# Picking the 256 best scores of a row: counting passes over the bits of the 256th score instead of rounds of eight maxima

## The chip, the cores and the metric

The kernel runs on one core of one Trainium2 chip. The metric is the device time of one execution in microseconds (us), the median of several. A core has a matrix engine (PE; its weight loads are listed as PEld), a vector engine (DVE), a scalar engine (ACT), a third elementwise engine (POOL) and a queue engine for transfers (SP). Each runs its own list of instructions in order; they meet at semaphores.

## The reference

One inference step of a two-layer encoder on 1024 new frames of one stream (the prompt) and 16 frames for each of 8 running streams (the sample; 2048 cached frames each). Layer 0 is a gated recurrence, layer 1 a sparse attention; both are followed by a feed-forward block. The change lies in the sparse attention. An indexer scores every key for every query, the best 256 keys of each query are kept, and ordinary attention runs over those:

```python
dots = jnp.einsum('bthd,bsd->bths', qib, ki_all, preferred_element_type=F32)
score = jnp.einsum('bth,bths->bts', wb.astype(F32), jax.nn.relu(dots))
score = jnp.where(admissible[None], score, -jnp.inf)
sel_val, sel_idx = lax.top_k(score, n_sel)          # n_sel = 256
valid = sel_val > -jnp.inf
...
logits = jnp.where(valid[:, :, None, None, :], logits, -jnp.inf)
p = jax.nn.softmax(logits, axis=-1).astype(vg.dtype)
```

A query of the prompt sees the keys of its own chunk of 64 frames and of the chunks before. `top_k` takes the lower index where scores tie.

## The kernel before, in words

The program is a chain of phases with a barrier between them: recurrence, feed-forward 0, projections, `select_phase`, `attend_prompt_phase`, `attend_sample_phase`, output projection, feed-forward 1, final norm. Queries lie on the 128 partitions. The prompt has 8 tiles of 128 queries, t = 0 to 7; tile t has (t+1)*128 keys. Tiles 0 and 1 have at most 256 keys and need no choice; tiles 2 to 7 do, and so does the sample, whose 128 queries have 2064 keys each (`score_s`). No key is gathered: the choice becomes an additive mask (`mask_p`, `mask_s`, 0 or a large negative number `NEG`), and attention runs over all keys.

**Choosing.** `top_step` is one step of the choice. A MAX8 finds the eight largest scores of each row, the next step replaces them by `TAKEN` (MATCH_REPLACE8), and so on; 64 steps (`STEPS`), 32 of each kind, mark 256 scores. `mask_from` turns the marks into the mask in one pass. Tiles go in pairs: (2,3) are `EARLY_TOP`, (4,5) and (6,7) are `LATE_TOP`, and the sample is alone. All of it runs on DVE.

**Where the steps stand in DVE's list.** In `select_phase` a loop over tiles 2 to 7 and 8 heads forms the prompt's scores: PE makes the dots (L1431 to L1433), ACT takes the relu into two buffers `se_relu_p` (L1476), DVE adds them up (L1533). In the 32 rounds of tiles 4 to 7 each round is followed by one step for the pair (2,3). After the loop DVE takes the remaining 32 steps of (2,3), their masks, and the first 8 steps of (4,5) (`LATE_STEPS_EARLY`), while PE and ACT score the sample (L1456, L1444, L1484, L1487), which needs nothing of DVE. The barrier follows. `attend_prompt_phase` starts with 6 more steps (`first_steps`) and then runs 64 blocks (tile t, pair of heads j), each of two halves: PE makes the logits (L1620 to L1622), DVE adds the mask and takes the row maximum (L1747, L1752, L1754), ACT takes the exponential (L1695), PE transposes (L1631), ACT copies (L1688), PE multiplies with the values (L1643), ACT scales (L1702, needs the reciprocal of DVE, L1737). PE keeps one half in hand: the logits of half u may only start when the maximum of half u-2 is out (`maxed`). The steps left are dealt out behind the halves by a table (`steps_by`), in proportion to t+3, so that the last of the sample's steps comes behind the last half.

Of the kernel before, what the change touches and what calls it, by code (L numbers as in the profile page):

```python
# [51 lines left out]
NEG = -1e30  # L52
# [1292 lines left out]
def mask_from(dve, mask, score):  # L1345

    return dve.tensor_scalar(mask, score, TAKEN * 0.7, NEG, ALU.is_gt, ALU.mult)


def select_phase(nc, env, x):  # L1350
# [35 lines left out]
    with ExitStack() as ctx:  # L1386
# [104 lines left out]
        def _(dve):  # L1491
# [29 lines left out]

            n = steps = 0
            for t in tiles:
                keys_n = (t + 1) * P
                score = score_p[:, score_at(t):score_at(t + 1)]
                for h in range(IDX_H):
                    w = wi[:, t, h:h + 1]
                    dve.wait_ge(p_relu, n + 1)
                    dve.drain()
                    if h == 0:  # L1530
                        dve.tensor_scalar(score, relu_p[:, n % 2, 0:keys_n], w, None, ALU.mult).then_inc(p_added, 1)
                    else:
                        dve.scalar_tensor_tensor(score, relu_p[:, n % 2, 0:keys_n], w, score, ALU.mult, ALU.add).then_inc(p_added, 1)  # L1533
                    n += 1
                    if t > EARLY_TOP[-1]:
                        top_step(dve, top, rows_of(EARLY_TOP), steps % 2)
                        steps += 1
                dve.drain()
                dve.memset(score_p[0:CHUNK, score_at(t + 1) - CHUNK:score_at(t + 1)], BARRED)
            dve.drain()  # L1540
            with dve.Fori(0, 4) as _:
                for step in range((STEPS - steps) // 4):
                    top_step(dve, top, rows_of(EARLY_TOP), step % 2)
            for t, score in zip(EARLY_TOP, rows_of(EARLY_TOP)):
# [4 lines left out]


def attend_prompt_phase(nc, env, x):
# [4 lines left out]
    mask_s, o_t, top, tail, other = env["mask_s"], env["o_t"], env["top"], env["tail"], env["other"]  # L1556
# [672 lines left out]
```

## Time and profile before

| | before |
|---|---|
| time, median of 3 runs | 4241.05 us (4238.36 to 4254.41) |
| span of the profiled execution | 4256.5 us |
| busy: PE, DVE, ACT, POOL | 3965.5, 2283.6, 1126.7, 220.7 us |
| mean granted clock of PE | 0.859 |

The times come from runs without the profiler, the profile from one further execution; its span, 4256.5 us, is 15.5 us over the median. A granted clock of 1.00 is PE's upper level, 2.4 GHz, and 0.50 its lower, 1.2 GHz. The busy shares are means over phases of quite different kinds: the feed-forward blocks, which the change doesn't touch, keep PE busy at full clock. What counts here are the 840 us from about 2150 to 2990 us of the span.

### The profile page before, as it was taken

The page shows a single profiled execution, that of the slowest core. Times are in us where ns is not written, and L with a number is a line of the kernel's source. Part 1 is how long each engine was busy: PE and PEld are TensorE (multiplying, and loading weights), DVE is VectorE, ACT ScalarE, POOL GpSimd, SP SyncE. Part 2 cuts the span into 40 slices and gives each one's busy share as a digit, 9 for nine tenths or more (in the row PEclk, how much of TensorE's full clock was granted, in tenths as well). Part 3 has the DMA queues.
Part 4 walks back from the last instruction along what each step waited for, and adds up shares of the span by engine and source line. Part 5 has one row for each costly group of instructions (what it writes and reads, how often), then busy time and mean ns, then how long its engine had stood idle before and what let it go on. Part 6 is the DMA issues. An engine that isn't in the chain of part 4 may idle for free. (4 is left out here: it accounts for less than half of the span.)

```text
span 4256.5 us, 57639 instructions
## 1 busy us (share of the span) xinstructions
PE 3965.5 (93%) x20761; PEld 3571.6 (84%) x20777; DVE 2283.6 (54%) x3818; ACT 1126.7 (26%) x2017; POOL 220.7 (5%) x300
## 2 busy tenths in 40 slices
PE   6999999987999999979978899999888899999998
PEld 5988888876999999969963678888447799999997
DVE  5455555545444444454477888877223444444445
ACT  4322222213111111122133433333332311112111
POOL 2000000003000000020000000000000200000000
PEclk8888888869999999999958555555999999999999
DMA  2111011001111111111212000000431011111111
GB/s 85 36 36 36 32 36 37 31 11 42 40 45 36 50 40 40 42 42 66 74 44 84 16 6 6 1 1 1 175 148 40 27 40 45 45 36 46 40 45 57
DMA packets 58083, 187.32 MB, mean 44 GB/s; under 512 B 6960, under 2 KB 23344, under 8 KB 53488
## 3 DMA queue, kind: packets, MB, share of 16 engines
q1 hardware_dynamic: 53184, 165.22, 11.2%
q0 software_dynamic: 4656, 18.65, 1.4%
q8 instruction: 178, 2.92, 0.3%
q14 instruction: 65, 0.53, 0.0%
HBM read 164.28 MB, written 19.57 MB: 43 GB/s over the span
## 5 line engine op out<-in xcount | busy, mean ns | idle before, releaser
L205 PE MATMUL ff0lin<-ff0h_hi,ff0w_hi 128*128 128x384 f32 x1056 | 356.1, 337 | 23.7 <-POOL ff0h_lo L163 15.4
L205 PE MATMUL ff1lin<-ff1h_hi,ff1w_hi 128*128 128x384 f32 x1056 | 356.7, 338 | 21.7 <-POOL ff1h_lo L163 13.8
L206 PE MATMUL ff1lin<-ff1h_lo,ff1w_hi 128*128 128x384 f32 x1056 | 356.1, 337 | 0.0
L207 PE MATMUL ff1lin<-ff1h_hi,ff1w_lo 128*128 128x384 f32 x1056 | 355.6, 337 | 0.0
L206 PE MATMUL ff0lin<-ff0h_lo,ff0w_hi 128*128 128x384 f32 x1056 | 355.2, 336 | 0.0
L207 PE MATMUL ff0lin<-ff0h_hi,ff0w_lo 128*128 128x384 f32 x1056 | 354.8, 336 | 0.0
L1643 PEld LDWEIGHTS ap_bank<-at_v,ap_probs_t 128*128 128x128 f32 x1152 | 258.6, 331 | 36.4 <-ACT ap_probs_t L1688 20.4
L205 PE MATMUL hg_lin<-hg_h_hi,hg_w_hi 128*128 128x384 f32 x768 | 271.1, 353 | 16.1 <-POOL hg_h_lo L163 14.2
L1643 PE MATMUL ap_bank<-at_v,ap_probs_t 128*128 128x64 f32 x1152 | 269.1, 418 | 10.2 <-ACT ap_probs_t L1688 10.1
L206 PE MATMUL hg_lin<-hg_h_lo,hg_w_hi 128*128 128x384 f32 x768 | 265.0, 345 | 0.0
L207 PE MATMUL hg_lin<-hg_h_hi,hg_w_lo 128*128 128x384 f32 x768 | 264.4, 344 | 0.0
L205 PEld LDWEIGHTS ff0lin<-ff0h_hi,ff0w_hi 128*128 128x128 f32 x1056 | 199.9, 189 | 26.1 <-POOL ff0h_lo L163 16.0
L205 PEld LDWEIGHTS ff1lin<-ff1h_hi,ff1w_hi 128*128 128x128 f32 x1056 | 200.6, 190 | 24.2 <-POOL ff1h_lo L163 14.4
L207 PEld LDWEIGHTS ff1lin<-ff1h_hi,ff1w_lo 128*128 128x128 f32 x1056 | 200.7, 190 | 0.0
L206 PEld LDWEIGHTS ff1lin<-ff1h_lo,ff1w_hi 128*128 128x128 f32 x1056 | 200.6, 190 | 0.0
L206 PEld LDWEIGHTS ff0lin<-ff0h_lo,ff0w_hi 128*128 128x128 f32 x1056 | 200.1, 190 | 0.0
L207 PEld LDWEIGHTS ff0lin<-ff0h_hi,ff0w_lo 128*128 128x128 f32 x1056 | 200.1, 189 | 0.0
L970 DVE TENSOR_TENSOR x<-x,ff1lin 128x384 f32<-128x384 f32 x264 | 141.2, 553 | 101.8 <-PE ff1lin L207 99.4
L970 DVE TENSOR_TENSOR x<-x,ff0lin 128x384 f32<-128x384 f32 x264 | 141.1, 553 | 101.8 <-PE ff0lin L207 99.4
L1695 ACT ACTIVATE ap_probs<-ap_probs,ap_neg_max 128x128 f32<-128x128 f32 (+7 forms) x128 | 99.2, 775 | 323.4 <-DVE ap_neg_max L1754 323.3
L205 PE MATMUL ff1lin<-ff1y_hi,ff1w_hi 128*128 128x384 f32 x528 | 180.0, 341 | 2.5 <-DVE ff1w_lo L199 2.5
L205 PE MATMUL ff0lin<-ff0y_hi,ff0w_hi 128*128 128x384 f32 x528 | 180.0, 341 | 2.5 <-DVE ff0w_lo L199 2.5
(328 smaller groups left out, 8767.4 us busy)
## 6 DMA issues: line engine op xcount, KB each, us to landing
ff0raw<-in_weights SPq DMA_DIRECT2D x66, 512.0 KB, 3.3
ff1raw<-in_weights SPq DMA_DIRECT2D x66, 512.0 KB, 3.2
hg_raw<-in_weights SPq DMA_DIRECT2D x40, 512.0 KB, 3.3
as_keys<-in_cache_k SPq DMA_DIRECT2D x16, 1024.0 KB, 4.8
as_vals<-in_cache_v SPq DMA_DIRECT2D x8, 2048.0 KB, 9.2
pj_raw<-in_weights SPq DMA_DIRECT2D x18, 512.0 KB, 3.9
se_keys<-in_cache_ki SPq DMA_DIRECT2D x8, 1024.0 KB, 4.7
x<-in_x SPq DMA_DIRECT2D x3, 1536.0 KB, 7.1
```

Source lines behind the costliest of these rows:

```text
L205: pe.matmul(out, w_hi, x_hi, start=start, stop=False)
L206: pe.matmul(out, w_hi, x_lo, start=False, stop=False)
L207: return pe.matmul(out, w_lo, x_hi, start=False, stop=stop)
L970: dve.tensor_tensor(xs, xs, lin[n % 6][:, 0:GT], ALU.add).then_inc(down_out, 1)
L1643: i = pe.matmul(ob[half][:, 0:HEAD_D], probs_t[:, half, c * P:(c + 1) * P], v_sb[:, c, col:col + HEAD_D], start=c == 0, stop=c == t)
L1695: act.activation(probs[:, half, 0:keys], probs[:, half, 0:keys], ACT.Exp, bias=neg_max[:, half], accum_out=total[:, half]).then_inc(exped, 1)
```

## The change

`top_step` and `mask_from` go; a class `Kth` takes their place. It finds the 256th largest score of each row by setting its bits from the top, one a step: count how many scores are at least the candidate, and take the bit back where fewer than 256 are. 32 steps (`STEPS`) fix all 32 bits. A step has a count for each row set, with the count read out of the accumulator, and two small instructions on [128 x 2] numbers, each behind the one before. Then `strictly_above` finds how many scores lie over the 256th, and `choose` makes the mask: scores above it are in, and of those equal to it as many as are still wanted, in order of index, by a running sum. The remaining steps for (2,3) and all 32 for (4,5) now stand in `select_phase`; (6,7) and the sample keep their place in the attention, 6 steps of (6,7) ahead of its first half.

```diff
-NEG = -1e30
+NEG = -2.0 ** 100
...
-STEPS = 2 * TOPK // 8
-LATE_STEPS_EARLY = 8
+STEPS = 32
+LATE_STEPS_EARLY = STEPS
...
-def top_step(dve, top, scores, taking):
-    for n, score in enumerate(scores):
-        if taking:
-            dve.match_replace(score, top[:, n, :], score, TAKEN)
-        else:
-            dve.max(top[:, n, :], score)
-    dve.drain()
...
-    return dve.tensor_scalar(mask, score, TAKEN * 0.7, NEG, ALU.is_gt, ALU.mult)
...
+    def step(self, dve, step, first, scores):
+        bit = STEPS - 1 - step
+        rows = slice(first, first + len(scores))
+        end = 0
+        for n, score in enumerate(scores):
+            row, start, end = first + n, end, end + score.shape[-1]
+            dve.tensor_scalar(self.flags[:, start:end], score, self.edge_of(row), None, ALU.is_ge, ALU.add,
+                              accum_out=self.counts[:, row, step:step + 1])
+        dve.drain()
+        dve.tensor_scalar(self.miss[:, rows], self.counts[:, rows, step], TOPK - 0.5, -1.0 if step == 0 else float(1 << bit),
+                          ALU.is_lt, ALU.mult)
+        dve.drain()
+        dve.scalar_tensor_tensor(self.edge[:, rows], self.edge[:, rows], (1 << bit) >> 1, self.miss[:, rows],
+                                 ALU.bitwise_xor, ALU.bitwise_xor)
+        dve.drain()
+
+    def strictly_above(self, dve, first, n):
+        rows = slice(first, first + n)
+        dve.scalar_tensor_tensor(self.over[:, rows, :], self.counts[:, rows, :], TOPK - 0.5, self.counts[:, rows, :],
+                                 ALU.is_lt, ALU.mult)
+        dve.drain()
+        dve.tensor_reduce(self.above[:, rows], self.over[:, rows, :], AX.X, ALU.max)
+        dve.drain()
+
+    def choose(self, dve, first, scores, parts):
...
+        for row, score, flag, masks in zip(rows, scores, flags, parts):
+            for mask, a, e in masks:
+                dve.tensor_scalar(mask, score[:, a:e], self.edge_of(row), NEG, ALU.is_le, ALU.mult)
+            dve.tensor_scalar(flag, score, self.edge_of(row), None, ALU.is_equal)
+        dve.drain()
+        for row, score, flag in zip(rows, scores, flags):
+            dve.tensor_tensor_scan(score, spread(self.one[:, 0:1], flag.shape), flag, self.above[:, row:row + 1], ALU.mult, ALU.add)
+        dve.drain()
+        for score, flag in zip(scores, flags):
+            dve.scalar_tensor_tensor(flag, score, TOPK + 0.5, flag, ALU.is_lt, ALU.mult)
+        dve.drain()
+        for flag, masks in zip(flags, parts):
+            for mask, a, e in masks:
+                dve.scalar_tensor_tensor(mask, flag[:, a:e], -NEG, mask, ALU.mult, ALU.add)
+        dve.drain()
...
                     if t > EARLY_TOP[-1]:
-                        top_step(dve, top, rows_of(EARLY_TOP), steps % 2)
+                        kth.step(dve, steps, 0, rows_of(EARLY_TOP))
                         steps += 1
...
-            with dve.Fori(0, 4) as _:
-                for step in range((STEPS - steps) // 4):
-                    top_step(dve, top, rows_of(EARLY_TOP), step % 2)
-            for t, score in zip(EARLY_TOP, rows_of(EARLY_TOP)):
-                mask_from(dve, mask_p[:, mask_at(t):mask_at(t + 1)], score)
-            with dve.Fori(0, 2) as _:
-                for step in range(LATE_STEPS_EARLY // 2):
-                    top_step(dve, top, rows_of(LATE_TOP[0:2]), step % 2)
+            for step in range(steps, STEPS):
+                kth.step(dve, step, 0, rows_of(EARLY_TOP))
+            masks_of(EARLY_TOP)
+            for step in range(LATE_STEPS_EARLY):
+                kth.step(dve, step, LATE_TOP[0] - FIRST_TOP, rows_of(LATE_TOP[0:2]))
+            masks_of(LATE_TOP[0:2])
```

Line numbers below L1320 move; a line of the functions around the change stands some 50 lines lower afterwards (L1533 is L1588, L1747 is L1797).

DVE's list in the scoring loop of `select_phase`, two rounds of tile 5 (`at_wi` are the head weights), before:

```order
L1533 SCALAR_TENSOR_TENSOR score_p<-se_relu_p,at_wi,score_p 128x768
L1341 MAX se_top<-score_p 128x8 x2
L1533 SCALAR_TENSOR_TENSOR score_p<-se_relu_p,at_wi,score_p 128x768
L1339 MATCH_REPLACE score_p<-se_top,score_p 128x384
L1339 MATCH_REPLACE score_p<-se_top,score_p 128x512
```

The same place in the changed kernel, one round of tile 4 and the start of the next:

```order
L1588 SCALAR_TENSOR_TENSOR score_p<-se_relu_p,at_wi,score_p 128x640
L1359 TENSOR_SCALAR kth_flags,kth_counts<-score_p,kth_edge 128x384
L1359 TENSOR_SCALAR kth_flags,kth_counts<-score_p,kth_edge 128x512
L1362 TENSOR_SCALAR kth_miss<-kth_counts 128x2
L1365 SCALAR_TENSOR_TENSOR kth_edge<-kth_edge,kth_miss 128x2
L1588 SCALAR_TENSOR_TENSOR score_p<-se_relu_p,at_wi,score_p 128x640
```

The step keeps its place behind each round; two small instructions, and the read of each accumulator (not listed), come to it. After the loop DVE's list of before ends, in the phase, with the masks of (2,3) and 8 steps for (4,5), of which the first two are shown:

```order
L1347 TENSOR_SCALAR mask_p<-score_p 128x384
L1347 TENSOR_SCALAR mask_p<-score_p 128x512
L1546 UNCONDITIONAL_BRANCH
L1341 MAX se_top<-score_p 128x8 x2
L1339 MATCH_REPLACE score_p<-se_top,score_p 128x640
L1339 MATCH_REPLACE score_p<-se_top,score_p 128x768
```

In the changed kernel this stands behind the loop: the choice for (2,3). Behind it follow 32 steps for (4,5) and then the same twelve rows with 640 and 768 elements:

```order
L1371 SCALAR_TENSOR_TENSOR kth_over<-kth_counts 128x64
L1374 TENSOR_REDUCE kth_above<-kth_over 128x2
L1383 TENSOR_SCALAR mask_p<-score_p,kth_edge 128x384
L1384 TENSOR_SCALAR kth_flags<-score_p,kth_edge 128x384
L1383 TENSOR_SCALAR mask_p<-score_p,kth_edge 128x512
L1384 TENSOR_SCALAR kth_flags<-score_p,kth_edge 128x512
L1387 SCALAR_TENSOR_TENSOR score_p<-kth_one,kth_above,kth_flags 128x384
L1387 SCALAR_TENSOR_TENSOR score_p<-kth_one,kth_above,kth_flags 128x512
L1390 SCALAR_TENSOR_TENSOR kth_flags<-score_p,kth_flags 128x384
L1390 SCALAR_TENSOR_TENSOR kth_flags<-score_p,kth_flags 128x512
L1394 SCALAR_TENSOR_TENSOR mask_p<-kth_flags,mask_p 128x384
L1394 SCALAR_TENSOR_TENSOR mask_p<-kth_flags,mask_p 128x512
```

Gone from here are the 32 remaining steps of (2,3), which are done inside the loop now. Come are the choice for both pairs (L1387 is its running sum) and all 32 steps of (4,5), of which only 8 of 64 stood here before. At the end of the attention DVE's list is, before:

```order
L1754 TENSOR_SCALAR ap_neg_max<-ap_part_max 128x1
L1737 RECIPROCAL ap_inv<-ap_total 128x1
L1341 MAX se_top<-score_s 128x8
L1339 MATCH_REPLACE score_s<-se_top,score_s 128x2064
L1347 TENSOR_SCALAR mask_s<-score_s 128x2048
L1347 TENSOR_SCALAR se_tail<-score_s 128x16
L1727 TENSOR_TENSOR mask_s<-se_tail,se_other 128x128
L1737 RECIPROCAL ap_inv<-ap_total 128x1
```

and in the changed kernel:

```order
L1804 TENSOR_SCALAR ap_neg_max<-ap_part_max 128x1
L1787 RECIPROCAL ap_inv<-ap_total 128x1
L1359 TENSOR_SCALAR kth_flags,kth_counts<-score_s,kth_edge 128x2064
L1362 TENSOR_SCALAR kth_miss<-kth_counts 128x1
L1365 SCALAR_TENSOR_TENSOR kth_edge<-kth_edge,kth_miss 128x1
...
L1383 TENSOR_SCALAR mask_s<-score_s,kth_edge 128x2048
L1383 TENSOR_SCALAR se_tail<-score_s,kth_edge 128x16
L1384 TENSOR_SCALAR kth_flags<-score_s,kth_edge 128x2064
L1387 SCALAR_TENSOR_TENSOR score_s<-kth_one,kth_above,kth_flags 128x2064
L1390 SCALAR_TENSOR_TENSOR kth_flags<-score_s,kth_flags 128x2064
L1394 SCALAR_TENSOR_TENSOR mask_s<-kth_flags,mask_s 128x2048
```

Two steps' work ahead of the last reciprocal becomes one step and the whole choice for the sample.

## Rows read from the trace of the kernel before

**Rows 1.** Stretches: length, busy PE, PEld, DVE, ACT, POOL, clock, DMA share, GB/s.

```profile
2150.00:2252.00 102.00, 92.46 (x258) 66.52 (x258) 88.46 (x172) 43.25 (x87) 0.00 (x0) 0.51 0.11 44
2252.00:2320.00 68.00, 65.93 (x227) 18.93 (x226) 53.44 (x122) 20.81 (x42) 0.00 (x0) 1.00 0.27 93
2331.00:2970.00 639.00, 624.25 (x2336) 513.10 (x2336) 522.59 (x1149) 239.92 (x642) 16.49 (x7) 0.50 0.02 6
```

**Rows 2.** Waits between 2150 and 2980 us: total, times, longest.

```profile
ACT se_relu_p L1476 <- DVE score_p L1533: 34.4, 26, 1.5
```

**Rows 3.** Timeline of DVE at the end of the scoring loop.

```profile
2247.69 1.15 DVE L1341 MAX8 se_top<-score_p 128x8 f32<-128x384 f32 x2
2248.98 1.28 DVE L1533 SCALAR_TENSOR_TENSOR score_p<-se_relu_p,at_wi,score_p 128x1024 f32<-128x1024 f32 x1
2250.18 0.08 DVE L1339 MATCH_VALUE_LOAD score_p<-se_top,score_p 128x8 f32 x1
...
2251.61 0.11 DVE L1539 MEMSET score_p<- 64x64 f32 x1 [0.16 <-issue]
```

**Rows 4.** Timeline of ACT at the end of the sample's scoring.

```profile
2317.97 2.14 ACT L1487 ACTIVATE score_s<-se_bank 128x512 f32<-128x512 f32 x5 [1.85 <-PE se_bank L1444]
```

**Rows 5.** Timeline of DVE across the barrier, to the attention's first half.

```profile
2320.41 1.69 DVE L1341 MAX8 se_top<-score_p 128x8 f32<-128x640 f32 x2 [10.85 <-PEq L1386]
...
2331.41 0.29 DVE L1747 CUSTOM_DVE_ANT_0 ap_probs<-ap_bank,mask_p 128x128 f32<-128x128 f32 x1
```

**Rows 6.** Groups of DVE instructions over the whole span, shapes apart.

```profile
L1938 DVE TENSOR_SCALAR_CACHE_REDUCE as_probs<-as_bank 128x512 f32<-128x512 f32 x64 | 44.3, 692 | 96.5 <-PE as_bank L1847 96.5
...
L551 DVE TENSOR_TENSOR_SCAN hg_G<-hg_keep,hg_tmp 128x1152 f32<-128x1152 bf16 x8 | 20.4, 2551 | 0.0
...
L1938 DVE TENSOR_SCALAR_CACHE_REDUCE as_probs<-as_bank 128x128 f32<-128x128 f32 x16 | 4.7, 291 | 4.6 <-PE as_bank L1847 4.6
...
L1531 DVE TENSOR_SCALAR score_p<-se_relu_p,at_wi 128x1024 f32<-128x1024 f32 x1 | 0.8, 754 | 0.1
```

**Rows 7.** Timeline of DVE in one half of tile 7.

```profile
2937.81 0.69 DVE L1747 CUSTOM_DVE_ANT_0 ap_probs<-ap_bank,mask_p 128x512 f32<-128x512 f32 x1
2938.42 0.08 DVE L1747 DVE_READ_ACCUMULATOR2_ANT ap_part_max<- 128x1 f32 x1
2938.58 0.16 DVE L1752 TENSOR_TENSOR ap_part_max<-ap_part_max 128x1 f32<-128x1 f32 x1
2938.82 0.15 DVE L1754 TENSOR_SCALAR ap_neg_max<-ap_part_max 128x1 f32<-128x1 f32 x1
2938.92 0.17 DVE L1737 RECIPROCAL ap_inv<-ap_total 128x1 f32<-128x1 f32 x1
```

**Rows 8.** Columns of rows 1, for tiles 0, 1, 2, 3 and 5 of the attention.

```profile
2330.00:2362.00 32.00, 26.80 (x100) 20.83 (x98) 21.37 (x86) 15.31 (x68) 2.35 (x1) 0.50 0.12 34
2362.00:2409.00 47.00, 40.28 (x150) 30.19 (x150) 41.91 (x120) 19.54 (x73) 2.35 (x1) 0.50 0.04 12
2409.00:2466.00 57.00, 54.50 (x193) 40.90 (x193) 51.60 (x134) 23.26 (x73) 2.35 (x1) 0.50 0.04 10
2466.00:2537.00 71.00, 70.81 (x251) 53.43 (x251) 61.58 (x128) 27.97 (x73) 2.36 (x1) 0.50 0.03 8
...
2624.00:2724.00 100.00, 100.00 (x388) 86.25 (x387) 82.64 (x186) 37.21 (x89) 2.36 (x1) 0.50 0.00 1
```

**Rows 9.** Timeline of PE in tile 5: logits and values of one half.

```profile
2702.71 0.79 PE L1620 MATMUL ap_bank<-ap_k_hi,ap_q_hi 64*128 64x512 f32 x1
...
2704.93 2.82 PE L1643 MATMUL ap_bank<-at_v,ap_probs_t 128*128 128x64 f32 x12
```

**Rows 10.** Timeline at the end of the attention, DVE and ACT.

```profile
2963.63 0.16 DVE L1737 RECIPROCAL ap_inv<-ap_total 128x1 f32<-128x1 f32 x1
...
2970.17 0.16 DVE L1737 RECIPROCAL ap_inv<-ap_total 128x1 f32<-128x1 f32 x1
...
2976.55 0.31 ACT L1702 ACTIVATE ap_o<-ap_bank,ap_inv 128x64 f32<-128x64 f32 x1 [3.76 <-PE ap_bank L1643]
```

More of the change, by code:

```diff
@@ L1323, with __init__, begin, edge_of @@
 LATE_TOP = range(FIRST_TOP + 2, PT)
-STEPS = 2 * TOPK // 8
-LATE_STEPS_EARLY = 8
+STEPS = 32
+LATE_STEPS_EARLY = STEPS
 def score_at(tile):
     return mask_at(tile) - mask_at(FIRST_TOP)
-def top_step(dve, top, scores, taking):
-    for n, score in enumerate(scores):
-        if taking:
-            dve.match_replace(score, top[:, n, :], score, TAKEN)
-        else:
-            dve.max(top[:, n, :], score)
-    dve.drain()
-def mask_from(dve, mask, score):
-    return dve.tensor_scalar(mask, score, TAKEN * 0.7, NEG, ALU.is_gt, ALU.mult)
+class Kth:
+    ROWS = PT - FIRST_TOP + 1
+    SAMPLE = ROWS - 1
+    def __init__(self, take):
+        self.edge, self.miss = take("kth_edge", [P, self.ROWS], I32), take("kth_miss", [P, self.ROWS], I32)
+        self.counts, self.over = take("kth_counts", [P, self.ROWS, STEPS]), take("kth_over", [P, self.ROWS, STEPS])
+        self.above = take("kth_above", [P, self.ROWS])
+        self.flags = take("kth_flags", [P, S_KEYS], BF16)
+        self.one = take("kth_one", [P, 2], BF16)
+    def begin(self, dve):
+        dve.memset(self.edge[:, :], 0)
+        dve.memset(self.one[:, :], 1.0)
+    def edge_of(self, row):
+        return self.edge[:, row:row + 1].bitcast(F32)
+    def step(self, dve, step, first, scores):
[21 more added lines that the diff above has]
+    def choose(self, dve, first, scores, parts):
+        ends = np.cumsum([score.shape[-1] for score in scores]).tolist()
+        flags = [self.flags[:, e - score.shape[-1]:e] for e, score in zip(ends, scores)]
+        rows = range(first, first + len(scores))
+        for row, score, flag, masks in zip(rows, scores, flags, parts):
[13 more added lines that the diff above has]
+        dve.drain()
@@ L1520, in rows_of, with masks_of @@
                 return [score_p[:, score_at(t):score_at(t + 1)] for t in ts]
+            def masks_of(ts):
+                kth.strictly_above(dve, ts[0] - FIRST_TOP, len(ts))
+                kth.choose(dve, ts[0] - FIRST_TOP, rows_of(ts), [[(mask_p[:, mask_at(t):mask_at(t + 1)], 0, (t + 1) * P)] for t in ts])
+            kth.begin(dve)
+            dve.drain()
             n = steps = 0
@@ L1555, in attend_prompt_phase @@
     k_sb, v_sb, mask_p = env["k"], env["v"], env["mask_p"]
[L1556 removed]
+    mask_s, o_t, kth, tail, other = env["mask_s"], env["o_t"], env["kth"], env["tail"], env["other"]
     score_p, score_s = env["score_p"], env["score_s"]
```

25 lines of the change are left out of this document (12 added, 13 removed).

## The prediction

> **What bounds the kernel now.** I read the busy times by stretch first, for the three phases that the steps of the choice lie in [rows 1]. In the scoring loop (2150 to 2252 us) DVE is busy 88 of 102 us, and it is the one waited for: ACT waits for DVE's sum to free a relu buffer 26 times, 34.4 us in all [rows 2]. A step put behind each round is therefore on the path there. In the next 68 us, the scoring of the sample, PE has 65.9 us and the upper clock, 1.00, and needs nothing of DVE. DVE is done early: it waits 10.85 us for the barrier [rows 5]. Then comes the attention, 639 us, with DVE busy 523 us and PE 624 us at a granted clock of 0.50. Taken by tile [rows 8], PE lacks 5.2, 6.7, 2.5 and 0.2 us in tiles 0 to 3 and nothing in tile 5. So some 14.6 us of the attention are waits of PE, nearly all ahead of 2466 us; that is all that the 639 less 624 us of the whole stretch leave. Behind that PE is the bound, at the lower clock, and DVE's steps run in its shadow.
>
> **What a step costs.** What counts is the distance from start to start. Before, a MAX8 step of (2,3) takes 1.29 us (2247.69 to 2248.98) and a MATCH step 1.43 us with 0.07 of the memset's wait in it (2250.18 to 2251.61) [rows 3]; I take 1.355 us as the mean.
>
> Now a count. The trace has no count over SBUF data. The nearest rows are L1938, a tensor_scalar with an accumulator, from PSUM: 691 less 291 ns for 384 elements more [rows 6], 1.04 ns an element. A tensor_scalar without an accumulator over SBUF data runs at half of that: L1531 takes 754 ns for 1024 elements [rows 6] where the sum L1533 of the same size takes 1.28 us [rows 3], 0.52 ns an element less. I take 1.04, since the accumulator is what the rows share, and keep 0.52 as the lower bound. For the fixed part the sum of L1533 starts 1.20 us ahead of its follower at 1024 elements (1.067 us of streaming) [rows 3]: 0.133 us with a per-row scalar, as the count has one; without it 0.61 - 0.53 = 0.08 us [rows 7]. Behind the last count come the read of the accumulator, then a small instruction after 0.16 us, the next after 0.24 [rows 7], and the next work after another 0.24: 0.64 us a step. Hence per step:
> - (2,3), 896 elements: 0.93 + 0.27 + 0.64 = 1.84 us (0.47 less at 0.52 ns)
> - (4,5), 1408: 1.47 + 0.27 + 0.64 = 2.37
> - (6,7), 1920: 2.00 + 0.27 + 0.64 = 2.91
> - sample, 2064: 2.15 + 0.13 + 0.64 = 2.92
>
> For (2,3) that is 0.5 us more than the step it replaces; there are half as many.
>
> **The choice** is a bigger piece than the mask pass of before. For (4,5): the two instructions on the counts 0.56 us; four passes without an accumulator at 0.52 ns, 2.0; the running sum, which the scan of L551 puts at 2551 ns for 1152 elements, or 2.08 ns each [rows 6], 3.3; two combining passes at 1.04 ns, 3.5: 9.4 us. (Of it the four passes are 4 x 704 x 0.52 and 0.13 each, and a drain is 0.1.) By the same terms 6.9 us for (2,3), 12.1 for (6,7), 12.6 for the sample.
>
> **Where it falls.**
> 1. Scoring loop: 32 steps on the path, (1.84 - 1.355) x 32 = +15.5 us.
> 2. Rest of the phase: DVE's list behind the loop becomes 6.9 + 32 x 2.37 + 9.4 = 92.2 us. Its cover, from the loop's end at 2251.7 [rows 3] to the end of ACT's last copy at 2320.1 [rows 4], is 68.4 us. What sticks out: +23.8 us. The 41 us of steps for (2,3) that go from here were hidden and give nothing back.
> 3. Ahead of the first half: six steps took 2331.4 - 2320.4 = 11.0 us [rows 5]; six of (6,7) take 17.4: +6.5. PE has had its logits ready by then, so all of it shows.
> 4. Attention: the table now deals out no step in tile 0, 2 in tile 1, 7 each in tiles 2 and 3, against 7, 18, 23 and 21. The 14.6 us of PE's waits nearly go; a little stays in tiles 0 and 1, where a half is a chain over all engines: -13. Some 200 us of DVE work vanish from the rest for nothing.
> 5. The choice for (6,7) comes in one piece, behind a half at the start of tile 5: 2.9 + 12.1 = 15.0 us, and the maximum of the next half needs 1.6 us more. PE can go on with one half. Logits take about 2.2 us of a half of 6.26 [rows 8, 9] and the maximum is out 1.7 us later, so the logits after next would start 12.5 - 3.9 = 8.6 us behind it; they start after 16.6: +8. Nothing catches this up, as PE is the bound.
> 6. The end: DVE's last reciprocal, which ACT's last scaling needs, came 6.5 us after 2963.6, and ACT was held by PE to 2976.5 [rows 10]. Now 2.9 + 12.6 + 0.3 us stand ahead of it: 2979.4, +3.
>
> Sum: 15.5 + 23.8 + 6.5 - 13 + 8 + 3 = +44 us. The sum is made against the profiled execution (span 4256.5 us); the median of the runs is 0.4% lower, which changes 44 us by nothing. So 4241 + 44 = **4285 us**. The other edits cost nothing: the value of NEG is a constant; the split copies of keys and queries move to the place of the attention's output, which is first written in the next phase; the loops written out spare DVE some 0.3 us each.
>
> **Two rules weighed.** L1938 shows 1.04 ns an element, but from PSUM [rows 6]. The Trainium skill (page "SBUF — State Buffer", section "Who interferes with whom") excludes from the two-port modes the tensor_scalar that also writes out its accumulator; by that rule the sum stands at +44 us, by the rate of the rows without accumulator at -3. No row here decides it.
>
> A [128 x 1] instruction takes 0.24 us to its follower behind a drain [rows 7]. The skill's page "VectorE: DVE Perf Modes", section on the TRN2 errata, has a table that gives it 58 cycles and one for each element, some 60 ns; by that the 70 steps on the path would be 25 us cheaper and the sum +19, an estimate. The row decides.
>
> **Rivals.**
> - *Counts at two elements a cycle* (0.52 ns; for it the rows without accumulator, against it that each accumulator row is at 1.04). The step of (2,3) costs 1.37 us (+0.5 over the loop), behind the loop 6.9 + 32 x 1.64 + 9.4 = 68.8 (+0.4), the six steps 11.5 (+0.5), tiles 0 to 3 -13, the choice +7, the end +2: -3 us, **4238**. Chance 0.10.
> - *The running total of a count goes at the scan's pace*, 2.08 ns [rows 6]; it also feeds each element's result into the next. Against it: the running maxima of L1938 and L1747 don't. It adds 0.93 x 32, 1.47 x 32, 2.0 x 6 and 4 us: +93 more, **4378**. Chance 0.05.
> - *The other side: PE's clock rises in the attention.* With PE's waits of tiles 0 and 1 gone the granted clock could reach its upper level. Then tiles 3 to 7, 504 us, would be bound by DVE and ACT: in tile 5 DVE needs some 2.2 us a half and 10/16 of a step of 2.9, 4.0 in place of 6.26 us. At that ratio -180 us: **4105**. It decides as soon as the clock rises at all. Against it: PE is busy 70.8 of 71 us in tile 3 and in full in tile 5, and the clock stays at 0.50 [rows 8]; what PE does there does not change. Chance 0.04.
> - *Small instructions cheaper than my 0.24 us*, or the work behind the loop better hidden: half of 25 us, and 5 us less for the choices: **4267**. Chance 0.10.
>
> **Numbers.** My forecast, counts at 1.04 ns, has the remaining 0.71, at 4285 with 4270 to 4300 as its own range (0.1 us on each of 70 steps is 7 us; the waits of tiles 0 to 3 may give 9 to 14.6; the choice's stall 0 to 10). The range 4257 to 4303 takes in that and the cheap small instructions, and leaves out the first three rivals, 0.19 together. About 0.5%, 21 us, is what a measurement of this kernel can tell from no change. Faster than 4220: 0.05 (the clock, a little of the first rival). Within: 0.18 (the first rival, half of the last, the low edge of the forecast). Slower than 4262: 0.77.
>
> **What would show it.** Right: L1359 at 128x1024 near 1285 ns and 2.37 us from count to count of (4,5); the attention's first maximum some 46 us later than at 2331; tile 0 some 4 us shorter; tiles 3, 4, 6, 7 unchanged in length at clock 0.50; one gap of PE of some 8 us in tile 5. The prediction is wrong if L1359 reads near 750 or 2350 ns, if the 32 steps of (4,5) end with PE still scoring the sample, or if a row of the attention shows a clock over 0.50 for long.

## The result and the profile after

The changed kernel took 4309.37 us (median of 4 runs, 4305.32 to 4312.39), the kernel before on the same chip 4247.73 us (4 runs): ratio 1.0133, 95% interval 1.0116 to 1.0150 (the ratio is the measured one, not the quotient of these two medians, which is 1.0145). It is slower, by 1.3%. Measured once more on another occasion (experiment 5) it was 4293.09 us against 4250.20: 1.0095, interval 1.0074 to 1.0116. What the likely reason for the two numbers is, is told below. The profiled execution of after is one of its timed ones (4309.97 us); its span is 4308.4 us, 51.9 us more than that of before. One run each of experiments 4, 6 and 9 was in a slow state, at 6052 to 10430 us, and is left out of their medians below.

Stretches of the changed kernel (same columns as rows 1): scoring loop, rest of the phase, ahead of the first maximum, then tiles 0, 1, 5 and 7.

```profile
2157.00:2267.00 110.00, 96.38 (x248) 64.42 (x246) 92.97 (x248) 39.14 (x81) 0.00 (x0) 0.51 0.03 10
2267.00:2361.00 94.00, 65.16 (x224) 18.76 (x222) 84.41 (x217) 20.94 (x42) 0.00 (x0) 0.87 0.19 67
2361.00:2385.00 24.00, 0.91 (x6) 0.72 (x6) 21.95 (x36) 4.25 (x3) 6.79 (x2) 0.50 0.25 66
2385.44:2412.68 27.24, 25.73 (x95) 20.21 (x96) 8.79 (x64) 15.24 (x68) 2.35 (x1) 0.50 0.07 20
2412.68:2453.89 41.21, 39.23 (x148) 29.75 (x149) 16.45 (x76) 20.36 (x73) 2.36 (x1) 0.50 0.05 14
2666.80:2776.11 109.31, 100.54 (x388) 86.30 (x389) 61.21 (x167) 36.97 (x89) 2.35 (x1) 0.50 0.00 1
2891.52:3013.81 122.29, 122.29 (x454) 101.63 (x454) 54.44 (x150) 40.80 (x83) 0.00 (x0) 0.50 0.00 1
```

Read them against [rows 1] and [rows 8]. DVE's busy time falls in all tiles (from 82.6 to 61.2 us in tile 5, 94.9 to 54.4 in tile 7), and tiles 6 and 7 are not a microsecond shorter for it, since PE fills them at the lower clock. What grows is the part ahead of tile 0. In the second stretch PE is busy 65 us as before, but the stretch is 94 us long, since DVE works for 84 of them. In the third PE has almost nothing to do for 24 us.

The groups of DVE instructions of the new choice, shapes apart:

```profile
L1359 DVE TENSOR_SCALAR_CACHE_REDUCE kth_flags<-score_s,kth_edge 128x2064 bf16<-128x2064 f32 x32 | 75.0, 2343 | 0.0
L1359 DVE TENSOR_SCALAR_CACHE_REDUCE kth_flags<-score_p,kth_edge 128x1024 bf16<-128x1024 f32 x32 | 40.8, 1275 | 0.0
L1359 DVE TENSOR_SCALAR_CACHE_REDUCE kth_flags<-score_p,kth_edge 128x512 bf16<-128x512 f32 x32 | 23.7, 742 | 0.0
...
L1387 DVE TENSOR_TENSOR_SCAN score_s<-kth_one,kth_above,kth_flags 128x2064 f32<-128x2064 bf16 x1 | 4.5, 4520 | 0.1
L1387 DVE TENSOR_TENSOR_SCAN score_p<-kth_one,kth_above,kth_flags 128x1024 f32<-128x1024 bf16 x1 | 2.3, 2323 | 0.0
...
L1383 DVE TENSOR_SCALAR mask_s<-score_s,kth_edge 128x2048 bf16<-128x2048 f32 x1 | 1.3, 1286 | 0.1
```

A count costs (1275 - 742) / 512 = 1.04 ns an element, the passes without accumulator half of it, the running sum about twice.

DVE from the end of the loop to the start of (4,5)'s steps. It answers to [rows 3]: a step is 3.10 us less the sum's 1.20 (2260.85 to 2263.95), 1.90 us.

```profile
2260.85 1.28 DVE L1588 SCALAR_TENSOR_TENSOR score_p<-se_relu_p,at_wi,score_p 128x1024 f32<-128x1024 f32 x1
2262.05 0.61 DVE L1359 TENSOR_SCALAR_CACHE_REDUCE kth_flags<-score_p,kth_edge 128x384 bf16<-128x384 f32 x1
...
2263.41 0.17 DVE L1362 TENSOR_SCALAR kth_miss<-kth_counts 128x2 int32<-128x2 f32 x1
2263.65 0.16 DVE L1365 SCALAR_TENSOR_TENSOR kth_edge<-kth_edge,kth_miss 128x2 int32<-128x2 int32 x1
2263.95 1.28 DVE L1588 SCALAR_TENSOR_TENSOR score_p<-se_relu_p,at_wi,score_p 128x1024 f32<-128x1024 f32 x1
...
2267.08 0.11 DVE L1594 MEMSET score_p<- 64x64 f32 x1 [0.16 <-issue]
2267.28 0.22 DVE L1371 SCALAR_TENSOR_TENSOR kth_over<-kth_counts 128x64 f32<-128x64 f32 x1
...
2274.24 0.88 DVE L1359 TENSOR_SCALAR_CACHE_REDUCE kth_flags<-score_p,kth_edge 128x640 bf16<-128x640 f32 x1
```

And across the barrier, DVE and then POOL, where [rows 5] had six steps in 11.0 us:

```profile
2361.55 1.15 DVE L1359 TENSOR_SCALAR_CACHE_REDUCE kth_flags<-score_p,kth_edge 128x896 bf16<-128x896 f32 x1 [0.39 <-PEq L1435]
...
2362.62 1.28 DVE L1359 TENSOR_SCALAR_CACHE_REDUCE kth_flags<-score_p,kth_edge 128x1024 bf16<-128x1024 f32 x1
...
2363.98 4.04 DVE L1362 TENSOR_SCALAR kth_miss<-kth_counts 128x2 int32<-128x2 f32 x1
2368.10 2.22 DVE L1365 SCALAR_TENSOR_TENSOR kth_edge<-kth_edge,kth_miss 128x2 int32<-128x2 int32 x1
2370.76 1.15 DVE L1359 TENSOR_SCALAR_CACHE_REDUCE kth_flags<-score_p,kth_edge 128x896 bf16<-128x896 f32 x1 [0.44 <-issue]
...
2385.44 0.29 DVE L1797 CUSTOM_DVE_ANT_0 ap_probs<-ap_bank,mask_p 128x128 f32<-128x128 f32 x1
```

```profile
2363.50 4.50 POOL L1657 TENSOR_TENSOR ap_k_lo<-at_k,ap_k_hi 128x2048 fp32r<-128x2048 f32 x1 [223.41 <-ACT ap_k_hi L1729]
2367.97 2.33 POOL L1660 TENSOR_TENSOR ap_q_lo<-ap_q,ap_q_hi 128x1024 fp32r<-128x1024 f32 x1
```

Two instructions on two numbers a row, 0.17 and 0.16 us as a rule, take 4.04 and 2.22 us here: each ends when an instruction of POOL ends. The same happens three times more in this execution, in tiles 2 to 4 (1.94, 2.16 and 2.36 us, at 2480.29, 2542.57 and 2620.55), each time to the end of one of POOL's subtractions of queries. The prediction had nothing of this.

**The account by stage**, in us. The marks are starts of instructions in the timelines: "loop" from the first weighted relu (2157.19 in after) to the last memset (2267.08), "behind" from there to ACT's split of the keys (2361.51), "lead" to the first maximum (2385.44), each tile to the first maximum of the next, tile 7 to its last maximum, "end" to the first transfer of the next phase (3033.42). E1 to E11 are the experiments below, one profiled execution each, which is one of their timed ones.

| | loop | behind | lead | tiles 0-3 | tile 4 | tile 5 | tile 6 | tile 7 | end | sum |
|---|---|---|---|---|---|---|---|---|---|---|
| before | 91.9 | 68.8 | 11.0 | 205.7 | 87.0 | 100.1 | 115.4 | 122.3 | 16.0 | 818.2 |
| after | 109.9 | 94.4 | 23.9 | 193.4 | 88.0 | 109.3 | 115.4 | 122.3 | 19.6 | 876.2 |
| E1 | 109.9 | 94.5 | 9.8 | 201.4 | 87.9 | 109.3 | 115.4 | 92.7 | 19.6 | 840.6 |
| E2 | 110.0 | 94.5 | 21.3 | 193.5 | 87.9 | 109.3 | 115.5 | 122.3 | 19.6 | 873.9 |
| E3 | 110.0 | 67.2 | 18.8 | 200.9 | 88.0 | 108.8 | 115.4 | 122.3 | 19.6 | 851.0 |
| E4 | 73.2 | 72.9 | 18.8 | 201.8 | 88.0 | 108.5 | 114.5 | 92.4 | 22.5 | 792.6 |
| E5 (after) | 109.9 | 94.5 | 23.9 | 193.5 | 87.9 | 109.3 | 115.4 | 110.0 | 19.6 | 864.1 |
| E6 | 109.9 | 95.5 | 23.6 | 193.1 | 88.0 | 100.1 | 115.4 | 109.3 | 19.3 | 854.0 |
| E7 | 73.6 | 72.6 | 9.8 | 189.9 | 87.9 | 100.1 | 115.4 | 87.2 | 14.5 | 751.1 |
| E8 | 73.6 | 71.7 | 9.8 | 193.5 | 88.0 | 100.1 | 115.4 | 109.3 | 18.1 | 779.5 |
| E9 (before) | 91.9 | 68.0 | 11.0 | 205.7 | 87.0 | 100.1 | 115.5 | 118.1 | 16.0 | 813.2 |
| E10 | 109.9 | 94.4 | 21.5 | 193.2 | 87.9 | 109.0 | 115.5 | 109.3 | 19.6 | 860.3 |
| E11 | 82.2 | 68.6 | 9.8 | 191.7 | 88.0 | 100.1 | 115.4 | 122.3 | 16.1 | 794.2 |

After less before is +58.0 us over these stages; the rest of the program was 6 us shorter in the one execution than in the other, which leaves the 51.9 us of the spans. Every stage but one repeats within 1 us where nothing in it was changed. The exception is tile 7.

### The profile page after: what moved, and what is told of

It reads as the page before. It is cut to its first block and busy times, and to the rows that moved or that the text cites. A ratio compares the mean times of both kernels' runs of the same rounds, so it can differ in the third digit from the quotient of the medians.

```text
span 4308.4 us, 57846 instructions
## 1 busy us (share of the span) xinstructions
PE 3959.0 (92%) x20761; PEld 3563.1 (83%) x20777; DVE 2142.9 (50%) x3889; ACT 1130.5 (26%) x2017; POOL 220.6 (5%) x300
## 5 line engine op out<-in xcount | busy, mean ns | idle before, releaser
L206 PE MATMUL hg_lin<-hg_h_hi,hg_w_hi 128*128 128x384 f32 x768 | 269.9, 351 | 17.4 <-POOL hg_h_lo L164 15.5
L1797 DVE CUSTOM_DVE_ANT_0 ap_probs<-ap_bank,mask_p 128x512 f32<-128x512 f32 (+3 forms) x192 | 102.0, 556 | 292.0 <-PE ap_bank L1675 289.6
```

Of the source, the lines that this page charges most:

```text
L206: pe.matmul(out, w_hi, x_hi, start=start, stop=False)
L1797: dve.tensor_tensor_reduce(out=probs[:, half, a:e], in0=qk[half][c][:, 0:e - a], in1=mask_p[:, mask_at(t) + a:mask_at(t) + e], scale=1.0, ...
```

## The experiments

**1 to 4: one edit each** (kernel before beside them: 4252.67 us). E1 drops the six steps ahead of the first half:

```diff
-    first_steps = steps_done + 6
+    first_steps = steps_done
```

> The changed kernel, but no step of the choice stands ahead of the attention's first half; the six of (6,7) are dealt out behind the halves with the rest. Theory (PE is the bound in the attention, DVE has room there): the first maximum comes when the logits are ready, some 9.5 us behind the barrier in place of 23.9, which gives 14.5 us; three or four steps of 2.9 us fall into tile 0, where they cost up to 3 us again. Net -11.5, about 4298 us where the changed kernel has 4309. Rival (the steps cost the same wherever they stand, since DVE is near its limit in tiles 0 to 3): within 3 us of 4309.

Measured: 4292.20 us, ratio 1.0100 (1.0079 to 1.0122). Lead 23.9 to 9.8 us; tiles 0 and 1 are 8.0 us longer, as the steps come back there. The six steps are worth 14.1 less 8.0 = 6 us net, where I had expected 11.5. Tile 7 was shorter by 30 us in the profiled execution, which no edit explains.

E2 takes POOL's subtraction of the keys and of the first queries to DVE, between the lead steps:

```diff
+            take_top(steps_done, steps_done + 1)
+            dve.wait_ge(k_hi_set, 1)
+            dve.tensor_tensor(k_lo[:, :, :], k_sb[:, :, 0:T_PROMPT], k_hi[:, :, :].bitcast(F32), ALU.subtract).then_inc(k_lo_set, 1)
```

> The changed kernel, but POOL's two subtractions at the start of the attention (the low part of the keys, 4.5 us, and of the first queries, 2.3 us) are done by DVE, between the six steps. Theory (the 4.04 us and 2.22 us that the small instructions L1362 and L1365 take in the first of these steps are a wait for POOL, which reads the same memory port): both fall to 0.17 us, DVE has 3.3 us of subtractions more, and the first maximum comes 21.3 us behind the barrier in place of 23.9: about -3 us, 4306. Rival 1 (they are slow because they are the first of their phase, code or ACT's work beside them): they stay at about 4 and 2 us, and the kernel gets 3 us slower, 4312.

DVE in the lead of E2:

```profile
2365.77 0.17 DVE L1362 TENSOR_SCALAR kth_miss<-kth_counts 128x2 int32<-128x2 f32 x1
2366.01 0.16 DVE L1365 SCALAR_TENSOR_TENSOR kth_edge<-kth_edge,kth_miss 128x2 int32<-128x2 int32 x1
2366.60 2.29 DVE L1784 TENSOR_TENSOR ap_k_lo<-at_k,ap_k_hi 128x2048 fp32r<-128x2048 f32 x1 [0.43 <-issue]
```

The small instructions are back at 0.17 and 0.16 us, and the lead is 21.3 us though DVE has 3.5 us more to do. So the 6 us in after are a wait for POOL. The time, 4286.66 us, ratio 1.0084 (1.0067 to 1.0101), was 20 us under the 4306 expected, while the profiled execution had 4308.7: the medians move by more than the stages do.

E3 leaves 12 of the 32 steps for (4,5), and their choice, to the attention (`LATE_STEPS_EARLY = 20`).

> The changed kernel with 20 of the 32 steps of the pair (4,5) in the selection phase; 12 steps and its choice go to the attention. Theory (the phase ends 25.7 us late because DVE's list behind the scoring loop is longer than the sample's scoring): DVE's list is 55 us against 69 us of cover, so all 25.7 us come back; the six steps ahead of the first half are of (4,5), -3 us; the choice for (4,5), 9.4 us in one piece, now stalls the halves of tile 1 by about 8 us and the added steps by 2: net -19, about 4290 us. Rival (something else holds the phase's end, or the work costs the same in the attention): within 5 us of 4309.

Measured: 4262.85 us, ratio 1.0023 (0.9996 to 1.0049), 27 us under what I expected. Its ten runs fall in two groups: five at 4242 to 4254 us, with a mean granted clock of 0.866 to 0.869, and five at 4272 to 4290 with 0.858 to 0.862. The profiled one, 4284.57 us, is in the second, and its stages are down by 25.2 us. Behind the loop 67.2 us: with 20 steps the list fits under the scoring of the sample, and the 26 us are gone. 7.5 us come back in tiles 0 to 3, where the choice for (4,5) stands in one piece now.

E4 has no step in the loop; all for (2,3) stand behind it, all for (4,5) in the attention.

```diff
-                    if t > EARLY_TOP[-1]:
-                        kth.step(dve, steps, 0, rows_of(EARLY_TOP))
-                        steps += 1
...
-LATE_STEPS_EARLY = STEPS
+LATE_STEPS_EARLY = 0
```

> The changed kernel with no step inside the scoring loop: the 32 steps of (2,3) and its choice stand behind the loop, the pair (4,5) goes to the attention as a whole (6 steps ahead of the first half). Theory (in the loop each step lies on the path, behind it 69 us are covered by the sample's scoring, and the attention has room): the loop becomes bound by PE and falls from 110 to about 84 us, DVE's list behind it is 32 x 1.90 + 6.9 = 68 us and just hidden (-25.7), -3 ahead of the first half, +12 for the choice in one piece and the denser steps in tiles 0 to 3: net -43, about 4266 us. Rival (the loop is bound by the chain from PE over ACT to DVE and not by the steps): the loop stays above 100 us and the kernel at 4280 or more.

Measured: 4249.04 us, ratio 0.9992 (0.9977 to 1.0007). The loop takes 73.2 us, some 10 less than I expected:

```profile
2165.00:2238.00 73.00, 70.30 (x232) 53.25 (x234) 43.90 (x53) 37.09 (x78) 0.00 (x0) 0.50 0.02 8
2238.00:2311.00 73.00, 70.51 (x238) 19.95 (x234) 58.40 (x205) 22.74 (x46) 0.00 (x0) 0.98 0.26 94
```

PE is busy 70.3 of 73.0 us there, so that is the loop's floor. The 32 steps in it cost (109.9 - 73.2) / 32 = 1.15 us each by the mark at the loop's end. Some of that comes back behind it: where DVE holds the loop up, ACT starts on the sample ahead of DVE's last memset (4.8 us in after and in E3), and in E4 it doesn't. Loop and rest together are 177.2 us in E3 and 146.1 in E4, so the price in the loop is 31 us, 0.97 us a step. Behind the loop (second row) the same steps cost nothing: DVE has 58 of 73 us, and the stretch has the length of PE's work.

**5: the changed kernel again**, unaltered.

> The changed kernel itself once more, to learn what its own scatter is. The runs so far showed that tile 7 of the attention took 122.3 us in the changed kernel and 92.5 us in two of its variants, because TensorE's granted clock went from 0.50 to 1.00 for some 45 us there. Theory A: such a rise comes by chance in any execution in which VectorE needs less than TensorE, so the changed kernel shows it as well: of its timed runs some lie at 4275 to 4295 us, the others at 4305 to 4312. Rival B: the rise needs something that only the variants have; then all runs lie at 4305 to 4312 us. The stages outside the attention are the same by both: loop 109.9, behind the loop 94.4, lead 23.9 us.

Its six runs went from 4278.70 to 4297.00 us: theory A in the main, though none of them lies at 4305 to 4312, where it had the others. Every stage repeats but tile 7, with 110.0 in place of 122.3 us. Three stretches around it in E5, columns as above:

```profile
2928.00:2934.00 6.00, 6.00 (x22) 4.62 (x20) 2.00 (x8) 1.42 (x3) 0.00 (x0) 0.50 0.00 0
2934.00:2952.00 18.00, 17.97 (x113) 14.97 (x112) 12.70 (x33) 8.80 (x20) 0.00 (x0) 0.92 0.00 1
2952.00:2958.00 6.00, 5.15 (x27) 4.53 (x26) 4.32 (x11) 2.89 (x7) 0.00 (x0) 0.67 0.00 0
```

PE is busy in full at 0.50, and without any gap the granted clock goes to 1.00 for some 17 us. It goes back after PE had gaps: it was busy 3.25 of the 4.10 us from 2950.00 to 2954.10, ahead of the fall.

**6: only the choice for (6,7) in pieces**, eight of them, one a half:

```diff
+    def pieces(self, dve, first, scores, parts):
...
+        return [lambda f=f, n=n, score=score, flag=flag, masks=masks: f(first + n, score, flag, masks)
+                for n, (score, flag, masks) in enumerate(zip(scores, flags, parts))
+                for f in (bounds, scan, kept, join)]
```

> The changed kernel with one term undone: the choice for tiles 6 and 7 (bounds, scan, ties, joining, 12.7 us in one piece at the start of tile 5) is issued as eight pieces, one in each of the halves after the last step, and the sample's steps that stood there follow later. My term: the first half of tile 5 falls from 17.2 to about 6.3 us and tile 5 from 109.3 to 100.3 us, 9 us off the whole, 4300 us where the clock stays at 0.50. Rival: VectorE's work is what counts, not its being in one piece; then eight halves are longer by 1 to 2 us each and tile 5 stays at 107 to 110 us. The choices for (2,3) and (4,5) are issued tile by tile too, each with some drains more: under 1 us behind the loop.

Tile 5 of E6, where after has the row 2666.80:2776.11 above:

```profile
2665.39:2765.49 100.10, 100.10 (x388) 86.25 (x389) 55.57 (x158) 37.36 (x89) 2.36 (x1) 0.50 0.00 1
```

109.3 to 100.1 us, PE busy in full. The work is the same; that it stood in one piece cost 9.2 us. The time was 4284.68 us, ratio 1.0083 (1.0055 to 1.0110).

**7: the attention without any step**, the floor. It leaves out the choices for tiles 4 to 7 and for the sample.

> Leaves out the choices for tiles 4 to 7 and for the sample: their masks are set to zero ahead of the attention, so VectorE has in the attention only the maxima and the reciprocals. In the scoring loop one step for (2,3) stands in every fourth round (8 in all), the other 24 and the choice for (2,3) behind it. My account: loop 73 us (steps hidden) or 82 us (at 1.15 us each, as the fourth experiment gives them per step), behind the loop 73, lead 9.8, tiles 27.2, 40, 53.7, 69.4, 87.9, 100.1, 115.4, 122.3 us at the lower clock, tail 16: about 88 us under the changed kernel, 4220 us. It is the floor for any way to deal the steps. Rival on the clock: if VectorE's load is what holds TensorE at 1.2 GHz, the clock rises in many tiles here and the attention falls by 100 us and more, to 4120 us or under.

Tiles 2, 5 and 7 of E7:

```profile
2382.79:2436.76 53.97, 53.97 (x196) 41.38 (x197) 13.33 (x64) 24.57 (x73) 2.35 (x1) 0.50 0.04 11
2594.25:2694.36 100.11, 100.11 (x388) 86.25 (x389) 23.59 (x113) 37.32 (x89) 2.36 (x1) 0.50 0.00 1
2809.77:2896.99 87.22, 87.09 (x454) 72.48 (x454) 26.12 (x106) 38.79 (x83) 0.00 (x0) 0.74 0.00 1
```

4225.13 us, ratio 0.9929 (0.9903 to 0.9954). With DVE busy 23.6 of 100 us tile 5 still takes 100.1 us at 0.50: DVE's load does not hold the clock down there. The rival falls. Of its nine runs seven took 4220 to 4227 us and two 4180 to 4188; the profiled one is of the two, so its 87.2 us for tile 7 are no floor of a usual run. The eight steps in the loop cost 0.4 us together.

**8: all of the work, dealt by DVE's free time.** One step for (2,3) in every fourth round of the loop, six for (4,5) behind it, none in the lead, one item a half later on, each choice in pieces:

```diff
+                    if t > EARLY_TOP[-1] and h % 4 == 1:
...
+            dealt = evenly(0) + evenly(6) + evenly(12) + evenly(16) + evenly(16) + [1] * 15 + [0]
+            dealt += [1, 1] + [1, 1, 2, 1, 1, 2, 1, 1, 2, 1, 1, 2, 1, 1] + [1, 2, 1, 1, 1, 1, 2, 1, 1, 1, 1, 1] + [1, 1, 1, 0]
```

> All of the reference's work, dealt by what VectorE has free in each half: in the loop one step for (2,3) in every fourth round, behind it the other 24, the choice for (2,3) and six steps for (4,5); no step ahead of the first maximum; none in tile 0, then 6, 12 and 8 steps for (4,5) in tiles 1 to 3, one item in each half of tiles 4 to 7 for the rest, each choice in pieces of 0.9 to 4.5 us. My account: the floor of the seventh experiment plus 2 us in each of tiles 1 to 3, plus 3 us at the end for the sample's last piece: 4228 us at the lower clock in the attention, and down to 4205 where the clock rises in tile 7: ratio 0.992 to 0.997 to the kernel before. Rival: a step of 2.4 us in a half with 1.4 to 2.1 us free delays the next maximum each time, 1 us for each of 18 steps in tiles 1 and 2, and the loop is longer by 9 us: 4245 to 4255 us, no faster than before.

4218.64 us, ratio **0.9928** (0.9907 to 0.9950): faster than both kernels, 32 us under before and some 75 us under after. The clock has little part in this: without tile 7 the stages add up to 670.2 us, where before has 695.9 and after 753.9. Tiles 4, 5 and 6 stand at the floor of E7, tiles 0 to 3 are 3.6 us over it, the end 3.6 us. The two times themselves can't rank E8 and E7: E8 does more work and has the lower median, with intervals that overlap.

**9: the kernel before again**, for its tile 7.

> The kernel before once more, for its profile: does TensorE's granted clock rise in tile 7 of the attention there too, and what is it worth? VectorE is busy 94.9 of 122.3 us in that tile, 6.3 us of the 8.2 us of a half, where the changed kernel needs 3.6. Theory A (the rise comes by chance in every kernel, and VectorE's work decides how much of it can be used): where it occurs, the halves fall from 8.2 to no less than 6.3 to 6.8 us, against 4.8 in the changed kernel, so that it brings 5 to 12 us, and the runs lie between 4237 and 4262 us. Rival B: a VectorE that is nearly full keeps the clock down; tile 7 takes 122.3 us in this profile and the spread is noise of other phases.

DVE in tile 7 of E9, two halves at the upper clock (maximum to maximum 6.73 us):

```profile
2937.39 0.69 DVE L1747 CUSTOM_DVE_ANT_0 ap_probs<-ap_bank,mask_p 128x512 f32<-128x512 f32 x1 [0.47 <-PE ap_bank L1622]
...
2939.20 2.29 DVE L1341 MAX8 se_top<-score_s 128x8 f32<-128x2064 f32 x1
...
2941.64 2.29 DVE L1339 MATCH_REPLACE8 score_s<-se_top,score_s 128x2064 f32<-128x2064 f32 x1
2944.12 0.69 DVE L1747 CUSTOM_DVE_ANT_0 ap_probs<-ap_bank,mask_p 128x512 f32<-128x512 f32 x1 [0.18 <-issue]
```

The clock rises here too, and DVE, with two steps a half, has no idle time left: the half falls from 8.2 to 6.7 us only, and the tile by 4.2 us, under the 5 to 12 that I expected. The time, 4245.51 us, against the runs of before beside it gives 0.9982 (0.9968 to 0.9995): so much can two sets of runs of one kernel differ. In E8 the same half falls to 4.80 us (2890.82 to 2895.62):

```profile
2890.82 0.69 DVE L1812 CUSTOM_DVE_ANT_0 ap_probs<-ap_bank,mask_p 128x512 f32<-128x512 f32 x1 [0.18 <-issue]
...
2892.63 2.34 DVE L1359 TENSOR_SCALAR_CACHE_REDUCE kth_flags<-score_s,kth_edge 128x2064 bf16<-128x2064 f32 x1
...
2895.62 0.69 DVE L1812 CUSTOM_DVE_ANT_0 ap_probs<-ap_bank,mask_p 128x512 f32<-128x512 f32 x1 [0.18 <-issue]
```

**10: which instruction waits for POOL.** In the lead the first small instruction runs once a tile:

```diff
+        for cols in [slice(n, n + 1) for n in range(rows.start, rows.stop)] if apart else [rows]:
```

> The changed kernel, but in the six steps ahead of the first maximum the small instruction that turns the counts into a miss runs once for each tile (128x1) in place of once for both (128x2). In the changed kernel it took 4.04 us on 128x2 while GpSimd subtracted keys (4.50 us), and the next, with two operands in SBUF, 2.22 us while GpSimd subtracted queries (2.33 us). In the same trace 128x1 instructions of this kind ran in 0.15 us beside GpSimd. Theory A (it is the form of the instruction that waits for GpSimd): the 128x1 instructions take 0.15 us, and the one with two operands behind them waits 6 us for both of GpSimd's in their place; the lead stays at 23.9 + 6 x 0.24 = 25.3 us. Rival B: any instruction of VectorE that is issued while GpSimd works waits; then the first 128x1 takes 4 us. Rival C: the wait went to whatever stood second in the step by chance of timing, and nothing waits: 19.3 us.

DVE in the lead of E10; POOL's subtraction of the keys ran from 2364.24 to 2368.74 us:

```profile
2364.72 0.21 DVE L1363 TENSOR_SCALAR kth_miss<-kth_counts 128x1 int32<-128x1 f32 x2
2365.01 3.75 DVE L1366 SCALAR_TENSOR_TENSOR kth_edge<-kth_edge,kth_miss 128x2 int32<-128x2 int32 x1
2368.86 1.15 DVE L1359 TENSOR_SCALAR_CACHE_REDUCE kth_flags<-score_p,kth_edge 128x896 bf16<-128x896 f32 x1
```

Theory A in kind: the form with one number a row ran beside POOL, the one with two operands waited. It waited for one of POOL's instructions, not both (3.75 us, not 6), so the lead was 21.5 us and not 25.3. The count behind it was issued inside POOL's second subtraction (2368.71 to 2371.04) and took its usual 1.15 us.

**11: 16 steps in the loop** (`h % 2 == 1`, twelve steps for (4,5) behind it, fewer in tiles 1 and 2), against E8.

> The dealt kernel of the eighth experiment with one step for (2,3) in every second round of the loop (16 in all, not 8), 16 behind it, twelve steps for (4,5) behind the loop (not six) and six fewer in tiles 1 and 2. In the loop 8 steps cost 0.4 us by the seventh and eighth experiments, 32 cost 36.6. If VectorE has slack in each round up to one step in two, the loop stays at 74 to 76 us, behind the loop 72, tiles 1 and 2 fall from 96.7 to 94.5 us: 4217 us, 1 to 2 under the eighth. If the price per step is reached already, the loop takes 82 us and the whole is 7 us over it: 4226 us.

4230.73 us, ratio 0.9953 (0.9938 to 0.9967). The loop takes 82.2 us: the price is there already, 8 steps are free and the next 8 cost 1.1 us each. Part of it comes back behind the loop (3.1 us) and in tiles 0 to 3 (1.8 us). Without tile 7, where only E8's profile shows the clock rise, the two kernels are 671.9 and 670.2 us: most of the 12 us between their medians is not the deal.

## Why the prediction came out as it did

The direction and the places were right, the size was not: +44 us on record, +58 by stage, and the first measurement lies 6 us over the range. The base moved too: I added to a median of 4241.05 us, and beside the changed kernel before had 4247.73, so 6.7 us of the distance from 4285 to 4309 are no term of mine. By its own steps:

1. *Scoring loop, +15.5.* Measured +18.0. A step was 1.90 us, not 1.84 (rows at 2260.85). The mechanism stands, but I did not see the slack beside it: the loop takes 73 us with no step and 74 with 8 (E4, E7). [Rows 1] hid it, since PE is shown busy nearly throughout: over the loop 88.7 of 91.9 us in before, while the same products fill 70.5 of 73.2 in E4. In a stage that others hold up, PE's busy time is not its need.
2. *Behind the loop, +23.8.* Measured +25.7. The list was 92.2 us by my sum, and took 94.4 with the barrier. The counts at 1.04 ns an element and the running sum at some 2.1 carried it, and E3 shows the cover: what fits under 68 us is free. By the rule that I took from the Trainium skill (page "SBUF — State Buffer", section "Who interferes with whom"), a tensor_scalar that writes its accumulator stays out of the two-port modes; the trace agrees, 1275 ns at 1024 elements against 748 for the pass without.
3. *The lead, +6.5.* Measured +12.9, and **this is the step that failed**. I took six steps of (6,7) at 2.91 us; five of them are that. The first took 9.2 us (2361.55 to 2370.76), since its two small instructions waited out POOL's subtractions. I had weighed that very page for the count and not for the instruction behind it, and I had not looked at what POOL does across the barrier. E2 and E10 show the cause. The same section of the Trainium skill's page says that a VectorE instruction in a two-port mode, or one with two inputs in SBUF, can't run beside a GpSimd instruction that reads SBUF: whichever is issued first holds the shared ports to its end. The trace agrees on the form with two inputs, 2.22 and 3.75 us. For the 4.04 us on 128x2 it agrees if that instruction ran in a two-port mode, which no row shows. The form on 128x1 ran on, two of them in 0.21 us.
4. *Tiles 0 to 3, -13.* Measured -12.2.
5. *The choice in tile 5, +8.* Measured +9.2 there, and E6 takes away exactly this. Tile 4 is 0.9 us longer as well, but that stays in E6 and in E7, which has no choice there: its cause is open.
6. *The end, +3.* Measured +3.6.

Of the 14 us missing, 6.4 are the lead with its wait for POOL; 2.5 the longer steps in the loop, 1.9 the phase behind it, 0.8 tiles 0 to 3, 2.1 tiles 4 and 5 and 0.6 the end. Only the first has a mechanism that was left out; the others, but for tile 4, are terms taken a little low. The three waits for POOL in tiles 2 to 4 cost little: none of these tiles is more than 1.6 us longer in after than in E7, which has no step there.

The rivals: counts at half the time and at the scan's pace both fall by the 1275 ns; "small instructions cheaper" falls by the 0.24 us between them, which held. *PE's clock rises* I gave 0.04. It happens, for other reasons and for less. The clock does rise, but only in tile 7, for 14 to 48 us, in some executions, in both kernels. Of the thirteen profiled executions here eight show it (E1, E4 to E10), and none in an earlier tile. It is the likely reason for the two ratios of the changed kernel: the mean granted clock of its runs was 0.855 to 0.858 where it gave 1.0133, and 0.859 to 0.864 where it gave 1.0095. The two groups of runs in E3 go with the granted clock in the same way. Only one run of each was profiled, so this is argued and not shown, and which chip the first measurement ran on is not known, so a difference between chips is not ruled out. In the profiles a rise is worth 30 us to a kernel that leaves DVE free (E1) and 4 us to before (E9). That it narrows the difference between the two kernels is not shown: the runs of before beside E5 reach from 4237 to 4261 us, with the clock from 0.867 down to 0.859, so that one profile need not be the most a rise gives it. The forecast's 44 us lie near the second measurement's 42.9 by luck: the sum was made for a kernel without a rise, where the stages say 58. What makes the clock rise stays open: VectorE's load doesn't (E7), PE was busy in full in the 30 us ahead of it in all eight, and its start lay between some 2855 and 2959 us of the span (E7, E6) in no visible relation to the edits.

So where did the gain go? 32 counting steps need less of DVE than 64 rounds: DVE's busy time falls from 2283.6 to 2142.9 us. Nearly all of it was taken off where PE is the bound, and the rest of (4,5)'s steps and two choices came to where nothing hides them. E8 has the same algorithm with another deal and gains 0.7%.

## What to carry to other kernels

Work on an engine that is not the bound costs by where it stands: 32 equal steps cost some 31 us in the loop and nothing behind it, and a choice of 12 us cost 9 in one piece and nothing in eight. Before moving work, write down for each stage how long the bounding engine takes alone, and fill each stage only up to it; a kernel that leaves the work out (E7) gives this floor in one run, stage by stage; its total says less where the clock varies from run to run. And when a stage has few instructions left, read every engine's row across it: a small VectorE instruction beside a long GpSimd one is where the prediction broke.

## What the runs showed of the hardware

- A VectorE instruction on two numbers a row took 4.04 us beside a GpSimd tensor_tensor of 4.50 us, one with two SBUF operands 2.22 and 3.75 us; two on one number a row took 0.21 us together, and a count with accumulator issued inside GpSimd's instruction took its usual 1.15 us (E10).
- Within the attention the granted clock of TensorE went from 0.50 to 1.00 with no gap in its work, only in tile 7 and only in eight of thirteen executions; ahead of each fall TensorE had gaps. The runs of one kernel spread over 18 to 48 us (E5, E7, E3), those of before over 12 to 25, more than most terms of the sum above.
- GpSimd takes 4.50 us for the subtraction of the keys, VectorE 2.29 us for the same (E2).
